# A hybrid diffusion trunk on one core: order of the first mixer's output stage, places of the modulation tiles, and the stage behind the recurrence

## The reference, cut to what matters

```python
def modulation(cvec, w_mod, b_mod):
    m = jax.nn.silu(cvec) @ w_mod + b_mod          # 1024 -> 6 * 1024, per layer

def mixer_ab(h, ...):                              # first layer
    u, v = gelu(z[..., :2 * A_DIM]) halves
    v = layernorm(v, v_g, v_b) by chunks of 128 tokens and 4 groups
    v = einsum('gpq,bnqgc->bnpgc', ws, v) + bs     # "mix", one per group g
    ya = u * v
    glu = zb[..., :B_DIM] * sigmoid(zb[..., B_DIM:])
    yb = silu(rmsnorm(dwconv(glu, conv_w, conv_b), norm_g))   # 31 taps
    return concatenate([ya, yb], -1) @ w_out

def rwkv_time_mix(...):                            # second layer, after the scan
    yn = (y - mean) * rsqrt(var + GN_EPS) * ln_g + ln_b       # per head
    out = (yn + bonus) * g
    # then concatenate([out, attention], -1) @ w_out
```

## Time and profile before

| | us |
|---|---|
| time, median of 3 runs (lowest to highest) | 1999.63 (1998.32 to 2001.02) |
| the profiled execution: its own time / its span | 2000.47 / 1998.6 |
| TensorE matmuls busy | 1884.6 (94%) |
| VectorE busy | 1061.9 (53%) |
| ScalarE busy | 768.8 (38%) |
| GpSimd busy | 598.1 (30%) |
| mean granted clock of TensorE | 0.974 |

### The profile page before, as it was taken

The page is one execution under the profiler, slowest core; times in us unless marked ns, Lnnn a source line. Parts: engine busy times, 40 slices in busy tenths (PEclk is TensorE's granted clock), DMA queues, the critical chain, the costliest instruction groups (busy, mean ns, idle before and its releaser), DMA issues.

```text
span 1998.6 us, 43869 instructions
## 1 busy us (share of the span) xinstructions
PE 1884.6 (94%) x18252; PEld 1730.5 (87%) x18252; DVE 1061.9 (53%) x1864; ACT 768.8 (38%) x1216; POOL 598.1 (30%) x327
## 2 busy tenths in 40 slices
PE   6899899999999998999998998989799999999996
PEld 3765699999999998878877887878699999999996
DVE  4497755442144547947566666666455443144423
ACT  4111335552155435237454232323144553145521
POOL 2300153444244445211111111111044444344442
PEclk8999899999999999899998999999899999999998
DMA  8666332222122221120110000000022222122221
GB/s 346 269 263 231 133 131 80 74 81 73 67 73 73 89 69 42 51 75 33 43 60 2 3 3 3 3 3 3 7 74 74 73 73 87 61 74 73 81 77 62
DMA packets 35344, 159.67 MB, mean 80 GB/s; under 512 B 3936, under 2 KB 4448, under 8 KB 28560
## 3 DMA queue, kind: packets, MB, share of 16 engines
q1 hardware_dynamic: 32832, 152.02, 20.9%
q10 hardware_dynamic: 1872, 3.61, 0.5%
q0 software_dynamic: 512, 2.13, 0.3%
HBM read 154.73 MB, written 3.01 MB: 79 GB/s over the span
## 4 chain that ended last, share of the span: by engine, by line
PE 83%; DVE 7%; ACT 3%; issue 3%; POOL 2%; DMA 2%; SPq 0%; DVEq 0%; PEldq 0%; POOLq 0%; ACTq 0%; PEld 0%
PE ps L220 18%; PE ps L222 18%; PE ps L221 18%; PE ps L1931 10%; PE ps L1970 2%; PE ps L706 2%; PE ps L696 2%; PE ps L1910 2%; PE ps L366 2%; DMA arena<-in_mod_w 2%; PE ps L1506 1%; PE ps L1227 1%; PE ps L1508 1%; PE ps L1507 1%; PE ps L2054 1%
## 5 line engine op out<-in xcount | busy, mean ns | idle before, releaser
L259 POOL TENSOR_TENSOR w_lo<-wslot,w_hi 128x1024 fp32r<-128x1024 f32 x130 | 319.7, 2460 | 690.5 <-ACT w_hi L254 690.5
L220 PE MATMUL ps<-xa_hi,w_hi 128*128 128x322 f32 (+1 forms) x1440 | 446.1, 310 | 0.0
L222 PE MATMUL ps<-xa_hi,w_lo 128*128 128x322 f32 (+1 forms) x1440 | 446.0, 310 | 0.0
L221 PE MATMUL ps<-xa_lo,w_hi 128*128 128x322 f32 (+1 forms) x1440 | 444.9, 309 | 0.0
L220 PEld LDWEIGHTS ps<-xa_hi,w_hi 128*128 128x128 f32 x1440 | 271.8, 189 | 0.2
L254 ACT ACTIVATE w_hi<-wslot 128x1024 fp32r<-128x1024 f32 x130 | 138.1, 1062 | 347.2 <-PE ps L222 289.8
L221 PEld LDWEIGHTS ps<-xa_lo,w_hi 128*128 128x128 f32 x1440 | 271.3, 188 | 0.2
L222 PEld LDWEIGHTS ps<-xa_hi,w_lo 128*128 128x128 f32 x1440 | 271.2, 188 | 0.0
L1931 PE MATMUL ps<-arena 64*64 64x64 f32 (+2 forms) x5760 | 243.3, 238 | 15.0 <-DVE arena L2238 12.6
L1931 PEld LDWEIGHTS ps<-arena 64*64 64x64 f32 x5760 | 214.5, 136 | 31.4 <-DVE arena L2238 16.7
L220 PE MATMUL ps<-hid_hi,d_hi 128*128 128x320 f32 x704 | 218.0, 310 | 3.9 <-POOL hid_lo L1106 3.9
(11 more groups left out here) (214 smaller groups left out, 3315.8 us busy)
## 6 DMA issues: line engine op xcount, KB each, us to landing
arena<-in_mod_w SPq DMA_DIRECT2D x48, 1024.0 KB, 7.1
wslot<-in_ffn_up SPq DMA_DIRECT2D x88, 512.0 KB, 3.5
wslot<-in_ffn_down SPq DMA_DIRECT2D x32, 704.0 KB, 4.0
wslot<-in_cd_w SPq DMA_DIRECT2D x22, 512.0 KB, 3.5
wslot<-in_w_out SPq DMA_DIRECT2D x16, 512.0 KB, 3.5
wslot<-in_ab_w SPq DMA_DIRECT2D x12, 512.0 KB, 8.1
x<-in_x_fm SPq DMA_DIRECT2D x2, 1280.0 KB, 7.3
out_y<-arena ACTq DMA_DIRECT2D x8, 320.0 KB, 2.4
```

Of the source, the lines that this page charges most:

```text
L220: nc.tensor.matmul(out, wh[:, m], hi[:, kk, t], start=(kk == 0), stop=False)
L221: nc.tensor.matmul(out, wh[:, m], lo[:, kk, t], start=False, stop=False)
L222: last = nc.tensor.matmul(out, wl[:, m], hi[:, kk, t], start=False, stop=(kk == k_all - 1))
L259: pool.tensor_tensor(wl[:, :], wslot[:, s, 0:tile_cols[base]], wh[:, :], ALU.subtract).then_inc(lo_ready, 1)
```

## The change

- **Modulation tiles.** One instead of two behind each glu tile; two behind each v tile as before; two behind each u tile; two between `mix(1)` and `mix(2)`; four between B and A of output tiles 0 and 1; two behind each of output tiles 2 to 5. ScalarE's, VectorE's and SP's parts move with them; two ring slots change place, and tile 46 waits for the norm of the convolution, whose input it overwrites.
- **First mixer's output.** B half first, then A. The sum of squares is moved ahead of the mixes; the last taps (13 in one loop) ahead of the layernorm's scaling; the norm of the convolution between mixes 1 and 2 on VectorE; all eight low parts behind mix 3, in the order 4 to 7, 0 to 3. Mixes 2 and 3 use banks 4 and 5.
- **Behind the recurrence.** The gate's product is made before the outputs and copied out by ScalarE; affine, bonus and gate become (y*ln_g*gate)*root + (bonus + ln_b)*gate, the first factor and the last term made before the root. The rows of w_out are turned on the host so that chunks 0 to 6 are attention and head pairs 0 to 2; ScalarE and GpSimd make their parts behind the last unit without a gate between the engines, and the last chunk's when it is there (`last_y`). One of two `pass_gate`s is left out.

```diff
-        mod(2 * n + 7, 2 * n + 8)
+        mod(n + 9)
...
     def mix(g):
-        pe.wait_ge(drained[g % 2], ab["out"] + 1)
-        if g >= 2:
-            pe.wait_ge(mix_used, g - 1)
+        if g < 2:
+            pe.wait_ge(drained[g], ab["out"] + 1)
+        elif g == 2:
+            pe.wait_ge(root_ready, 2)
+        else:
+            pe.wait_ge(mix_used, 3)
...
-            last = product_of_parts(ab["out"], n, [kk], KD, y_hi, y_lo)
-        if KD - 1 in ks:
+            last = product_of_parts(ab["out"], n, [kk], KD, y_hi, y_lo, first=KA, end=KA - 1)
+        if KA - 1 in ks:
             last.then_inc(product, 1)
...
     for n in range(GLU_TILES):
         glu_tile(n)
-        if n % 2 == 0 and n:
-            mod_columns_pe(pe, n // 2 + 1)
-        mod_pe(pe, 8 + 2 * n, 9 + 2 * n)
+        if n == 6:
+            mod_columns_pe(pe, 2)
+        mod_pe(pe, 8 + n)
...
         v_tile(t)
         if t % 2 == 0:
-            mod_columns_pe(pe, 5 + t // 2)
-        mod_pe(pe, 24 + 2 * t, 25 + 2 * t)
-    for n, js in enumerate(((34, 35), (36, 37), (38,), (39,))):
+            mod_columns_pe(pe, 3 + t // 2)
+        mod_pe(pe, 16 + 2 * t, 17 + 2 * t)
+    for n in range(4):
         u_tile(n)
-        if n == 1:
-            mod_columns_pe(pe, 8)
-        mod_pe(pe, *js)
+        if n % 2:
+            mod_columns_pe(pe, 6 + n // 2)
+        mod_pe(pe, 26 + 2 * n, 27 + 2 * n)
+    pe.wait_ge(vtm_ready, NT)
+    rms_pe(pe, KD, KA)
     pe.wait_ge(vmul_ready, NT)
-    pe.wait_ge(vtm_ready, NT)
     mix(0)
     mix(1)
-    rms_pe(pe, KD, KA)
-    mod_columns_pe(pe, 9)
+    mod_pe(pe, 34, 35)
     mix(2)
     mix(3)
-    pe.wait_ge(mix_used, 3)
+    pe.wait_ge(mix_used, 1)
+    out_part(0, range(KA, KD), True)
+    pe.wait_ge(mix_used, 2)
+    out_part(1, range(KA, KD), False)
+    mod_columns_pe(pe, 8)
+    mod_pe(pe, 36, 37, 38, 39)
+    pe.wait_ge(mix_used, 4)
     out_part(0, range(KA), True)
-    pe.wait_ge(mix_used, 4)
     out_part(1, range(KA), False)
-    mod_pe(pe, 40, 41, 42, 43)
-    out_part(0, range(KA, KD), True)
-    out_part(1, range(KA, KD), False)
     for n in range(2, KD):
         out_tile(n)
-        if n == 2:
-            mod_columns_pe(pe, 10)
-        if n < 4:
-            mod_pe(pe, 40 + 2 * n, 41 + 2 * n)
-        if n == 4:
-            mod_columns_pe(pe, 11)
+        if n in (2, 4, 6):
+            mod_columns_pe(pe, 8 + n // 2)
+        if n < 6:
+            mod_pe(pe, 36 + 2 * n, 37 + 2 * n)
     pe.wait_ge(root_ready, 2)
 def mix_bank(g):
-    return 2 * (g % 2)
+    return (0, 2, 4, 4)[g]
...
         gate_of_glu(i)
         if i < GLU_TILES // 2 - 1:
             tile_hi(act, glu, i + 1, 1)
-        mod_act(act, 2 + i)
+        if i == 2:
+            mod_act(act, 2)
...
     for t in range(NT):
+        if t % 2 == 0:
+            mod_act(act, 3 + t // 2)
         gelu_of_v(t)
-        if t % 2:
-            mod_act(act, 6 + t // 2)
...
-    gelu_of_u(0)
-    mod_act(act, 8)
-    gelu_of_u(1)
     act.wait_ge(var_ready, 1)
...
     warm(act, ACT.Gelu_apprx_tanh)
+    gelu_of_u(0)
+    mod_act(act, 6)
+    gelu_of_u(1)
     gelu_of_u(2)
+    mod_act(act, 7)
+    tile_hi(act, ab["out"], 0, 0)
     gelu_of_u(3)
-    mod_act(act, 9)
-    for s in range(2):
-        tile_hi(act, ab["out"], 0, s)
     squares_of_conv(1)
     root_act(act, 1, KA, 0)
     warm(act, ACT.Silu)
     for k in range(KA):
-        act.wait_ge(ya_ready, k + 1)
-        nc.scalar.activation(y_hi[:, k, :], ycat[:, k, :], ACT.Copy).then_inc(src_hi, 1)
-    for k in range(KA):
+        if k == 2:
+            tile_hi(act, ab["out"], 0, 1)
+            mod_act(act, 8)
         act.wait_ge(yn_ready, k + 1)
         nc.scalar.activation(ycat[:, KA + k, :], ycat[:, KA + k, :], ACT.Silu,
                              scale=pcol("b_norm", k)).then_inc(yb_ready, 1)
         act.wait_ge(yb_ready, k + 1)
         nc.scalar.activation(y_hi[:, KA + k, :], ycat[:, KA + k, :], ACT.Copy).then_inc(src_hi, 1)
+    for k in range(KA):
+        act.wait_ge(ya_ready, k + 1)
+        nc.scalar.activation(y_hi[:, k, :], ycat[:, k, :], ACT.Copy).then_inc(src_hi, 1)
     for n in range(KD):
         i, s = n // 2, n % 2
         if n < KD - 2:
@@ -855,8 +874,8 @@
         if n == 0:
             act.wait_ge(mod_done, 6)
         xa_hi_of(act, 0, n)
-        if n in (1, 3):
-            mod_act(act, 10 + n // 2)
+        if n in (1, 3, 5):
...
     first_tap(0)
     taps(6, {0: 1})
     after_low_part_of(4)
-    taps(7, {0: 7})
+    taps(3, {0: 7})
     gated(1)
-    mod_dve(dve, st, 2)
+    taps(4, {0: 10})
     after_low_part_of(5)
     first_tap(1)
     taps(3, {0: 14, 1: 1})
     after_low_part_of(6)
     taps(4, {0: 17, 1: 4})
     gated(2)
-    mod_dve(dve, st, 3)
     after_low_part_of(7)
...
     gated(3)
-    mod_dve(dve, st, 4)
+    mod_dve(dve, st, 2)
...
+    mod_dve(dve, st, 3)
     taps(5, {1: 22, 2: 5, 3: 5})
-    mod_dve(dve, st, 6)
+    mod_dve(dve, st, 4)
...
-    mod_dve(dve, st, 7)
-    taps(4, {2: 18, 3: 18})
+    mod_dve(dve, st, 5)
+    taps(13, {2: 18, 3: 18})
+    st.wait()
+    dve.sem_inc(conv_ready, 1)
...
-    taps(9, {2: 22, 3: 22})
-    st.wait()
-    dve.sem_inc(conv_ready, 1)
+    mod_dve(dve, st, 6)
+    def norm_of_conv():
+        rms_dve(dve, st, 1)
+        for k in range(KA):
+            for a, b, v in GROUPS:
+                last = nc.vector.tensor_tensor(ycat[:, KA + k, a:b], conv[:, k, a + PAD * v:b + PAD * v], rs[:, a:b], ALU.mult)
+            last.then_inc(yn_ready, 1)
...
+    def y_lo_of(k):
+        if k >= KA:
+            dve.wait_ge(mix_ready, 4)
+        else:
+            dve.wait_ge(ya_ready, KA)
+        dve.wait_ge(src_hi, KD + Y_ORDER.index(k) + 1)
+        nc.vector.tensor_tensor(y_lo[:, k, :], ycat[:, k, :], y_hi[:, k, :], ALU.subtract).then_inc(src_lo["dve"], 1)
     for g in range(4):
+        if g == 2:
+            norm_of_conv()
+            mod_dve(dve, st, 7)
...
-    mod_dve(dve, st, 9)
-    for k in range(KA):
-        dve.wait_ge(ya_ready, k + 1)
-    source_lo(dve, "dve", KD, ycat, y_hi, y_lo, range(KA))
-    rms_dve(dve, st, 1)
-    for k in range(KA):
-        for a, b, v in GROUPS:
-            last = nc.vector.tensor_tensor(ycat[:, KA + k, a:b], conv[:, k, a + PAD * v:b + PAD * v], rs[:, a:b], ALU.mult)
-        last.then_inc(yn_ready, 1)
-    source_lo(dve, "dve", KD, ycat, y_hi, y_lo, range(KA, KD))
+    for k in Y_ORDER:
+        y_lo_of(k)
+    mod_dve(dve, st, 8)
     for n in range(KD):
         residual_of(dve, ab["out"], 2 * KD, n // 2, n % 2)
         xa_lo_of(dve, 0, n)
-        if n in (3, 5):
-            mod_dve(dve, st, 10 + n // 4)
+        if n in (2, 4, 6):
+            mod_dve(dve, st, 8 + n // 2)
...
+    todo += [(END, [("gate", "act", 2), ("mean", "dve", 2), ("var", "act", 2)])]
...
     for r in range(ROUNDS):
         chain(LAST, r)
+    for g in range(2):
+        round_of((END, "gate", g), scan_w[:, HP - 1, 2 * P:3 * P], lg)
     outputs(LAST)
...
-    for g in range(2):
-        round_of((END, "gate", g), scan_w[:, HP - 1, 2 * P:3 * P], lg)
+    wait(emptied["act"], entry[END, "var", 1][2])
+    wait(emptied["dve"], entry[END, "mean", 1][2])
...
+    wait(emptied["dve"], entry[LAST, "RM", 2][2])
+    tile_hi(act, cd["out"], 0, 0)
+    tile_hi(act, cd["out"], 0, 1)
+    for n in range(KD - 1):
+        nc.scalar.activation(y1_hi[:, n, :], ycat1[:, Y1_OF[n], :], ACT.Copy).then_inc(src_hi, 1)
+    for g in range(2):
+        take_bank((END, "gate", g), half(last_gate, g), half_bank((END, "gate", g)))
     tail_square(END, HP - 1)
     tail_root(END)
+    act.wait_ge(last_y, 1)
+    nc.scalar.activation(y1_hi[:, KD - 1, :], ycat1[:, Y1_OF[KD - 1], :], ACT.Copy).then_inc(src_hi, 1)
...
+Y1_OF = (4, 5, 6, 7, 0, 1, 2, 3)
+last_gate = rkv[:, 0, :]
+last_y = sem("last_y")
...
+    y, bonus = ycat1[:, HP - 1, :], rkv[:, KA + HP - 1, :]
+    wait(emptied["act"], entry[END, "gate", 1][2])
+    wait(emptied["dve"], entry[LAST, "bonus", 1][2])
+    wait(emptied["dve"], entry[END, "mean", 1][2])
+    st(nc.vector.scalar_tensor_tensor(out=bonus, in0=bonus, scalar=pcol("ln_b", HP - 1), in1=last_gate, op0=ALU.add, op1=ALU.mult))
+    st.wait()
+    st(nc.vector.scalar_tensor_tensor(out=last_gate, in0=y, scalar=pcol("ln_g", HP - 1), in1=last_gate, op0=ALU.mult, op1=ALU.mult))
     for part in range(4):
         tail_root(END, part)
-    tail_norm(END, HP - 1)
-    tail_affine(HP - 1)
-    tail_add(HP - 1)
-    tail_gate(END, HP - 1)
+    st.wait()
+    wait(tail_sq, HP)
+    st(nc.vector.tensor_tensor(y, last_gate, rs[:, :], ALU.mult))
+    st.wait()
+    nc.vector.tensor_tensor(y, y, bonus, ALU.add).then_inc(last_y, 1)
...
     pool.dma_start(io["new_state"], fins).then_inc(fin_out, 16)
+    tile_lo(pool, cd["out"], 0, 0)
+    for n in range(KD - 1):
+        pool.wait_ge(src_hi, 3 * KD + n + 1)
+        pool.tensor_tensor(y1_lo[:, n, :], ycat1[:, Y1_OF[n], :], y1_hi[:, n, :], ALU.subtract).then_inc(src_lo["pool"], 1)
     pool.wait_ge(fin_out, 16)
```

(36 more changed lines are left out.)

55 lines of the change are left out of this document (27 added, 28 removed).

## The result

The changed kernel is slower: 2008.36 us median (2006.85 to 2010.99, 6 runs) against 1999.93 (1998.32 to 2001.02, 6 runs), a ratio of 1.0046 with a 95% interval of 1.0035 to 1.0057. I had forecast 1995.8 and given "slower" 0.12.

A forecast was written before the change was run, and what follows sets the result against it. TensorE, busy 1884.6 of 1998.6 us, was taken as the bound, with gains only from its idle or lower-clock time. Mixer +5.8 and tail -9.6 made -3.8 against the median 1999.63: 1995.8 us, range 1988.5 to 2002.

The forecast's parts named there:

- Both signs of being wrong: First mixer's first output matmul starting before 224 or after 232; or the recurrence's tail giving under 7 us.
- Tail, step 4 and 5: Behind the recurrence: VectorE's products and last low part, partly beside GpSimd's weight tile; eighth chunk ends 1452.0, 9.6 us less.
- Steps 1 to 3: Behind the recurrence: gate matmuls delay outputs 1.2 us, roots at 1441.4; ScalarE's copies hidden; GpSimd's low parts 1433.4 to 1446.
- the paragraph on the two folded instructions: Recurrence's tail: VectorE's two folded instructions each wait for at most one GpSimd low part, both done by 1441.7.
- the other case: Recurrence's tail: GpSimd keeps its turn through all seven low parts, folded instructions end at 1446.2, gain 5 us, not 9.6.
- Mixer up to the sum of squares: First mixer up to the mixes: TensorE ready at 204.8, 8.4 us earlier, with six modulation tiles in debt.
- The wait in front of glu tile 7: First mixer: TensorE wants pair 2's bank at 104.2, VectorE's gating frees it at 107.4; 3.2 us lost.
- From there to the output: First mixer, sum of squares through mixes and norm to the first low part: 204.8 to 228.0, against 226.60 before.
- The modulation debt: First mixer's output: more modulation tiles and transposes left to do, 4.4 us more; the 3.14 us fourth-tile wait stays.
- R3: Rival, slower: GpSimd and VectorE meetings in the tail (4.6 us) and among mixes and taps; +9.2, 2005; chance 0.12 shared, own 0.08.
- R2: Rival: mixer loses what the tail gives, VectorE late in gating, TensorE ready at 208; +9.5 - 9.6, 1999.5; chance 0.23.

The follow-up runs named there:

- experiment 4: Kernel before with only the new recurrence tail, plus GpSimd waiting behind its third low part until VectorE's folded instructions are done: 1991.62 us, ratio 0.9956.
- Experiment 5: Changed kernel with VectorE gating pair 2 ahead of its four taps instead of behind them: 2005.39 us, ratio 1.0033 to the kernel before.
- Experiments 6 and 7: Changed kernel with modulation tiles 36 and 37 between mixes 2 and 3: 1996.91 us; changed kernel with A half first again, new tile spread kept: 1999.68 us.
- experiment 2: Kernel before with only the first mixer changed (order, modulation tiles), old recurrence tail kept: 2010.91 us, ratio 1.0047.

## Why the prediction was wrong, step by step

Both signs of being wrong that I had named came: the first output matmul at 233.65, later than 232, and a tail that gives 3.5, under 7.

**Tail, step 4 and 5: 9.6 forecast, 3.5 in the profile, 3.0 by the medians.** Steps 1 to 3 held, but for the roots: I had them 11.9 us behind the chain's last step and they landed 9.9 behind it (1448.72 + 1.06). ScalarE's parts were hidden (they begin at 1435.46, 4.4 us ahead of the chain's last step), GpSimd began its seven 4.0 us behind that step (3.9 forecast) and needed 1.51 each, not 1.67, and TensorE started when the roots were read.

The step that failed is the choice in the paragraph on the two folded instructions: each waits for one low part at most. I took that reading of the Trainium skill (SBUF — State Buffer, "Who interferes with whom") for 9.6, and had the other case in the text ("if GpSimd kept its turn through all seven", 5 us). It kept it: 7.95 and 7.82 us, against 1.76 with a wait in between and 0.97 when it was through. For the folded instruction the trace doesn't agree with the reading that VectorE gets the lock after one instruction of a back-to-back row; for L961 in the kernel before and for L2428 in experiment 4 it does. So the reading held for those two and failed where the sum hung on it. The tile's first residual then came 27.4 us behind the chain's last step instead of 32.6: 5.2 us less, the 5 of the other case. Another 1.7 went in the restart: behind the 7.30 us pause TensorE ran at half clock to about 1470.6 (matmuls 0.27 us apart), into the second tile. I had charged a slow restart to the start of the tile only.

**Mixer up to the sum of squares: ready at 204.8 forecast, 209.9 measured.** The wait in front of glu tile 7 was there as forecast, 4.70 us and not 3.2. Its restart was missing from my sum: that tile took 9.8 us instead of 7.2. And 0.9 is a later start of this execution (its first product starts at 42.64, the old one's at 41.75). 1.5 + 2.6 + 0.9 are 5.0 of the 5.1. Experiment 5 shows that taking this wait away alone moves it to modulation tile 16; even a right price for it was no price of the edit.

**From there to the output: 23.2 us forecast, 23.7 measured** (209.93 to 233.65). This part held, and so did the place of the idle time. One term of it was too small: for mix 3 and its way back the sum has 1.8, neither the 1.3 of full clock nor the 2.4 of half clock that the text gives, and it took 2.5 (228.37 to 230.91). But I took the idle time as a delay of the output only. Experiments 6 and 7 show that it is the main cost: filled or undone, the mixer loses some 3 us or less.

**The modulation debt: 4.4 forecast, 6.9 measured** (first output matmul to sum of x 75.6 before, 82.5 after). The load wait for the fourth tile in a row didn't stay at 3.14, it became 4.97, with a slow restart. In experiment 2, with the same mixer, it was 3.20 and the debt 5.6 (233.09 to 314.27), so part of this miss belongs to the one execution.

Sum for the mixer: 5.8 + 5.1 + 0.5 + 2.5 = 13.9, which is the 14.0 of the traces. The medians of experiment 2 give 9.4; the 0.9 of the start and the 1.8 of the longer load wait are not in every execution.

**The rivals.** R3, the meetings of GpSimd and VectorE, had the mechanism of the tail and a chance of 0.08; its price for the tail, 4.6, is near the 4.4 of the hold. R2 had the mixer's direction. What came was both at once, 6 us lost in one and 8 in the other. No case had that combination: R3 had the hold in the tail, but meetings of VectorE and GpSimd in the mixer, where restarts and the load wait came instead. The cases shared an error: most stalls were priced at their length.
